# RWKV steps: one bank and one eviction for the 64x64 results of both chunks, and the newer tile first in a round

## The chip, the core and the metric

The kernel runs on one core of a Trainium2 chip. A core has five engines that run their own instruction queues in order: TensorE (matmuls, written PE, its weight loads PEld), VectorE (DVE), ScalarE (ACT), GpSimd (POOL) and SyncE (SP, which issues DMAs). They wait for each other with semaphores. TensorE writes its results to PSUM, eight banks of 128 partitions x 512 fp32; VectorE or ScalarE then move them to SBUF, which is called an eviction here. The metric is the device time of the whole kernel in microseconds; lower is better.

## The reference

Everything is fp32. The model is a mixer block (attention, an RG-LRU, an RWKV-7 recurrence), then two further layers with experts. The change touches the RWKV part alone, for one sequence of 1024 tokens and 4 heads of 64:

```python
def step(state, inp):
    r_t, w_t, k_t, v_t, kk_t, b_t = inp
    sa = jnp.einsum("bhvk,bhk->bhv", state, -kk_t)
    state = (state * w_t[:, :, None, :] + sa[..., None] * b_t[:, :, None, :]
             + v_t[..., None] * k_t[:, :, None, :])
    y_t = jnp.einsum("bhvk,bhk->bhv", state, r_t)
    return state, y_t
...
_, y = lax.scan(step, s0, (tm(rh), tm(wh), tm(kh), tm(vh), tm(kk), tm(bh)))
```

## The kernel before, in words

The recurrence is computed in chunks of 64 tokens (`CH`). Within a chunk it becomes products of 64x64 matrices and the inverse of a triangular one, found by repeated squaring. A tile is 128 tokens, that is two chunks: chunk 0 lies on partitions 0 to 63, chunk 1 on 64 to 127 (`HALVES`). There are eight tiles (`NT`).

A tile goes through 20 steps. Steps 0 to 9 are its front: `ab`, `tok` (0), `p2` (1), `kr` (2), `p4`, `x1` (3), `p8`, `x2` (4), `akv`, `x3` (5), `xt` (6), `q32` (7), `pb` (8), `q64` (9). They do not need the state. Steps 10 to 18 are its back: `x64` (10), `gt`, `u0` (11), `sv0` (12), `dv0`, `ys0` (13), `sv1` (14), `dv1`, `ys1` (15), `yc` (16), `mean` (17), `var` (18), and in step 19 VectorE alone takes the reciprocal of the deviation (L1341) and multiplies by it (L1343). The state passes from chunk to chunk through `sv`, SA (L1304, VectorE), `dv` and the new state (L1315).

`rounds()` (L973) sets the order for TensorE, ScalarE and VectorE alike: in round r = 10 i + s the back step 10 + s of tile i - 1 comes first, then the front step s of tile i. Each of the three engines runs its own function over these rounds: `pe_rwkv` (L1007), `act_rwkv` (L1171), `dve_rwkv` (L1224). While tile 0 is in work, ScalarE and VectorE also run pieces of the RG-LRU (`act_lru`, `dve_lru`), after each step of tile 0.

`by_chunk` (L1016) issues a step's products, for each head q once on the rows of chunk 0 and once on those of chunk 1, each of the two with a PSUM bank of its own. A matmul reads one chunk's rows and writes the same half of the partitions. The bank of chunk 0 and that of chunk 1 are then evicted by two operations on 64 partitions each: `chunk` (L1182, recorded at `copy`, L1180) on ScalarE, `combine` (L1247, recorded at L1252) and `chunk1` (L1254, recorded at L1257) on VectorE. For `p2` and `p4`, which hold two products, ScalarE takes chunk 0 and VectorE chunk 1. `by_parity` (L1039) does `ab` and `kr`; their evictions are L1239 and L1245 (masks).

The banks are two rings, `fr` of four banks for the front and `bk_` of four for the back. A key of a ring gets its bank by its place in FRONT or BACK (L959, L963), and a matmul waits until the key four places earlier is evicted. All matmuls of the stage but `tok` (L1061) are recorded at L202. Each fp32 matmul leaves two records in the trace for the matmul and two for the weight load.

Of the kernel before, what the change touches and what calls it, by code (L numbers as in the profile page):

```python
# [18 lines left out]
NT = T // P  # L19
HD = 64  # L20
AH, AKV = 8, 2
# [4 lines left out]
CH = 64  # L26
# [144 lines left out]
def build(nc, io):  # L171
    ctx = ExitStack()
    with ctx:
# [7 lines left out]
        V, S, G = signal("dve_own"), signal("act_own"), signal("pool_own")  # L181
# [22 lines left out]
        def wait_all(e, points):  # L204
            for point in points:
                e.wait_ge(*point)
# [476 lines left out]
        mN, id64, mT3, mU3 = take(CH), take(CH), take(3, CH), take(3, CH)  # L683
# [264 lines left out]
        def tile_set():  # L948
# [10 lines left out]
        FRONT = [("ab0", "V"), ("ab1", "V"), ("tok0", "S"), ("tok1", "S"), ("p2_0", "S"), ("p2_1", "V"), ("kr0", "V"), ("kr1", "V"),  # L959
# [3 lines left out]
        BACK = [("x64_0", "V"), ("x64_1", "V"), ("gt_0", "S"), ("gt_1", "S"), ("u0_0", "S"), ("u0_1", "S")]  # L963
# [9 lines left out]
        def rounds():  # L973

            for r in range(10 * (NT + 1)):
                i, s = divmod(r, 10)
                if i:
                    yield i - 1, 10 + s
                if i < NT:
                    yield i, s  # L980
# [26 lines left out]
        def pe_rwkv(e):  # L1007
            wait_all(e, after_prep)
            for i, s in rounds():
# [6 lines left out]
                def by_chunk(ring, name, products, *after):  # L1016

                    wait_all(e, after)
                    keys = [(i, f"{name}_{c}") for c in range(2)]
                    for key in keys:  # L1020
                        wait_all(e, ring.free(key))
                    for g, (lhs, rhs) in enumerate(products):
                        for q in range(4):
                            for c, cr in enumerate(HALVES):
                                o = ring.bank[keys[c]][cr, 4 * CH * g + CH * q:4 * CH * g + CH * (q + 1)]
                                m = mm(e, o, lhs(q)[cr], rhs(q)[cr], True, True)
                                if (g, q) == (len(products) - 1, 3):
                                    m.then_inc(*ring.fill(keys[c]))

                def of(t):  # L1030
                    return lambda q: t[:, q, :]
# [3 lines left out]

                def both(name):
                    return [fr.empty((i, f"{name}_{c}")) for c in range(2)]
# [25 lines left out]
                elif s == 1:  # L1063
                    by_chunk(fr, "p2", [(of(NT_), of(N)), (of(N), of(NT_))], fr.empty((i, "ab0")), fr.empty((i, "ab1")))
                elif s == 2:
                    by_parity("kr", [(Kf, Af), (Bf, Rf), (Kf, Rf)])
                elif s == 3:
                    by_chunk(fr, "p4", [(of(PTA), of(PA)), (of(PA), of(PTA))], *both("p2"))
                    by_chunk(fr, "x1", [(of(PA), of(XTa))])
                elif s == 4:  # L1070
                    by_chunk(fr, "p8", [(of(PTB), of(PB))], *both("p4"))
                    by_chunk(fr, "x2", [(of(PB), of(XTb))], *both("x1"))
                elif s == 5:
                    by_chunk(fr, "akv", [(of(AKT), tok(3))], fr.empty((i, "kr1")))
                    by_chunk(fr, "x3", [(of(PA), of(XTa))], *both("p8"), *both("x2"))
                elif s == 6:
                    by_chunk(fr, "xt", [(of(XTb), lambda q: id64)], *both("x3"))
                elif s == 7:
                    by_chunk(fr, "q32", [(of(CT32), of(X_))], *both("xt"))
                elif s == 8:  # L1080
                    by_chunk(fr, "pb", [(of(XTb), of(Q)), (of(Q), of(XTb))], *both("q32"))
                elif s == 9:
                    by_chunk(fr, "q64", [(of(CT64), of(XB))], *both("pb"))
                elif s == 10:
                    by_chunk(bk_, "x64", [(of(Q), of(XTa))], *both("q64"))
                elif s == 11:
                    for c in range(2):
                        e.wait_ge(*bk_.empty((i, f"x64_{c}")))
# [10 lines left out]
                    by_chunk(bk_, "u0", [(of(XTb), of(AKV))], *both("akv"))  # L1099
# [64 lines left out]
        def side(ap, cr, n):  # L1164

            return ap[cr, 0:CH * n].rearrange("p (a b) -> p a b", a=n)

        def flat(ap):
            return ap.rearrange("p a b c -> p (a b) c")

        def act_rwkv(e):  # L1171
            wait_all(e, after_prep)
            for i, s in rounds():
                own = sets[i % 2]
                tk, GT, AKV, U0, Q = (own[n] for n in ("tok", "GT", "akv", "u0", "Q"))
                cols = slice(P * i, P * (i + 1))

                def copy(ring, name, dst, src):
                    e.wait_ge(*ring.full((i, name)))
                    e.activation(dst, src, ACT.Copy, bias=0.0).then_inc(*ring.drain((i, name), "S"))  # L1180

                def chunk(ring, name, c, dst, n):  # L1182
                    copy(ring, f"{name}_{c}", dst[HALVES[c]], side(ring.bank[i, f"{name}_{c}"], HALVES[c], n))

                if s == 0:
                    if i == 1:
                        e.wait_ge(*lru_u.at(2))
                    for half in range(2):
                        copy(fr, f"tok{half}", tk[:, 4 * half:4 * half + 4, :], four(fr.bank[i, f"tok{half}"]))
                elif s == 1:  # L1190
                    chunk(fr, "p2", 0, flat(own["P1"]), 8)
                elif s == 3:
                    chunk(fr, "p4", 0, flat(own["P2"]), 8)
                elif s == 4:
                    for c in range(2):
                        chunk(fr, "p8", c, own["P1"][:, 0], 4)
                elif s == 5:
                    for c in range(2):
                        chunk(fr, "akv", c, AKV, 4)
                elif s == 6:  # L1200
                    for c in range(2):
                        chunk(fr, "xt", c, own["X1"][:, 0], 4)
                elif s in (7, 9):
                    for c in range(2):
                        chunk(fr, "q32" if s == 7 else "q64", c, Q, 4)
                elif s == 11:
                    for c in range(2):
                        copy(bk_, f"gt_{c}", GT[:, :, HALVES[c]], two(bk_.bank[i, f"gt_{c}"], CH))
                    for c in range(2):
                        chunk(bk_, "u0", c, U0, 4)  # L1210
# [12 lines left out]

        def dve_rwkv(e):  # L1224
# [4 lines left out]
            for i, s in rounds():  # L1229
# [17 lines left out]
                def combine(ring, name, dst, src, op, n=4):  # L1247

                    for c, cr in enumerate(HALVES):
                        key = (i, f"{name}_{c}")  # L1250
                        e.wait_ge(*ring.full(key))
                        e.tensor_tensor(dst[cr], src[cr], side(ring.bank[key], cr, n), op).then_inc(*ring.drain(key, "V"))  # L1252

                def chunk1(name, dst):  # L1254
                    key = (i, f"{name}_1")
                    e.wait_ge(*fr.full(key))
                    e.tensor_copy(flat(dst)[HALVES[1]], side(fr.bank[key], HALVES[1], 8)).then_inc(*fr.drain(key, "V"))  # L1257
# [10 lines left out]
                elif s == 1:  # L1268
                    e.wait_ge(*fr.empty((i, "ab1")))
                    e.tensor_tensor(X2[:, 1], own["T3"][:, 0], bc_mid(id64, 4), ALU.add).then_inc(*V.up())  # L1270
                    chunk1("p2", own["P1"])
# [4 lines left out]
                elif s == 3:  # L1276
                    chunk1("p4", own["P2"])
                    e.wait_ge(*V.last())
                    combine(fr, "x1", X1[:, 1], X2[:, 1], ALU.add)
                elif s == 4:  # L1280
                    for c in range(2):
                        e.wait_ge(*fr.empty((i, f"x1_{c}")))
                    combine(fr, "x2", X2[:, 1], X1[:, 1], ALU.add)
                elif s == 5:
                    for c in range(2):
                        e.wait_ge(*fr.empty((i, f"x2_{c}")))
                    combine(fr, "x3", X1[:, 1], X2[:, 1], ALU.add)
                elif s == 8:
                    for c in range(2):
                        e.wait_ge(*fr.empty((i, f"xt_{c}")))  # L1290
                        e.wait_ge(*fr.empty((i, f"x3_{c}")))
                    combine(fr, "pb", flat(X2), flat(X1), ALU.subtract, 8)
                elif s == 10:
                    for c in range(2):
                        e.wait_ge(*fr.empty((i, f"pb_{c}")))
                    combine(bk_, "x64", X1[:, 1], X2[:, 1], ALU.subtract)
                elif s in (12, 14):
                    c = (s - 12) // 2
                    cr = HALVES[c]
                    e.wait_ge(*bk_.empty((i, f"u0_{c}")))  # L1300
# [1725 lines left out]
```

## Time and profile before

| what | us |
|---|---|
| median of 3 runs | 2386.47 (2379.73 to 2386.75) |
| the profiled execution | 2384.51 |
| its span, first to last instruction | 2382.8 |
| TensorE busy | 2136.5 (90%) |
| VectorE busy | 852.3 (36%) |
| ScalarE busy | 580.0 (24%) |
| GpSimd busy | 198.0 (8%) |
| mean granted TensorE clock | 0.940 of full |

The rows further down come from this one profiled execution. Times are microseconds from the span's start unless marked ns. In the view in order of time, like instructions that follow each other are merged: the row has the start, the length from the first start to the last end, the engine, the line, the operation and the count, and in brackets how long the engine stood idle before it and what ended that. Matmuls are pipelined, so a busy TensorE is not TensorE at its peak.

### The profile page before, as it was taken

The page shows a single profiled execution, that of the slowest core. Times are in us where ns is not written, and L with a number is a line of the kernel's source. Part 1 is how long each engine was busy: PE and PEld are TensorE (multiplying, and loading weights), DVE is VectorE, ACT ScalarE, POOL GpSimd, SP SyncE. Part 2 cuts the span into 40 slices and gives each one's busy share as a digit, 9 for nine tenths or more (in the row PEclk, how much of TensorE's full clock was granted, in tenths as well). Part 3 has the DMA queues.
Part 4 walks back from the last instruction along what each step waited for, and adds up shares of the span by engine and source line. Part 5 has one row for each costly group of instructions (what it writes and reads, how often), then busy time and mean ns, then how long its engine had stood idle before and what let it go on. Part 6 is the DMA issues. An engine that isn't in the chain of part 4 may idle for free. (4 is left out here: it accounts for less than half of the span.)

```text
span 2382.8 us, 27540 instructions
## 1 busy us (share of the span) xinstructions
PE 2136.5 (90%) x10876; PEld 1236.1 (52%) x10876; DVE 852.3 (36%) x1873; ACT 580.0 (24%) x1397; POOL 198.0 (8%) x297
## 2 busy tenths in 40 slices
PE   8999999777797949999995999999999949999991
PEld 4545554677444824444443656777764424444440
DVE  1116648766143441111123543443441141112115
ACT  1013334344011301111221433333331111111112
POOL 0000002010242200000001100000000000000002
PEclk9999999799798969999997999999999959999996
DMA  3500000000211147999975100000010057999976
GB/s 124 212 23 36 18 2 3 2 3 3 107 53 40 54 184 293 365 411 377 372 298 191 55 1 1 1 1 1 27 57 27 27 203 295 369 372 370 366 283 239
DMA packets 46200, 349.30 MB, mean 147 GB/s; under 512 B 6256, under 2 KB 6576, under 8 KB 36208
## 3 DMA queue, kind: packets, MB, share of 16 engines
q1 hardware_dynamic: 32176, 296.97, 31.9%
q0 software_dynamic: 13888, 50.47, 6.0%
q8 instruction: 92, 1.51, 0.3%
q14 instruction: 44, 0.36, 0.0%
HBM read 292.82 MB, written 54.59 MB: 146 GB/s over the span
## 5 line engine op out<-in xcount | busy, mean ns | idle before, releaser
L202 PE MATMUL psum<-arena 128*128 128x512 f32 (+7 forms) x9328 | 1976.2, 389 | 147.7 <-DVE arena L1920 25.9
L202 PEld LDWEIGHTS psum<-arena 128*128 128x128 f32 (+3 forms) x9328 | 1062.1, 174 | 992.4 <-issue 842.9
L2051 DVE TENSOR_TENSOR arena<-psum,arena 128x256 f32<-128x256 f32 x64 | 27.2, 425 | 541.0 <-ACT arena L2095 541.0
L2131 POOL DMA_INDIRECT arena<-xn_rows,arena x64 | 60.2, 941 | 819.9 <-PE psum L2018 589.2
L2095 ACT ACTIVATE arena<-psum 128x256 f32<-128x256 f32 x64 | 24.6, 384 | 402.0 <-PE psum L202 402.0
L1472 ACT ACTIVATE arena<-arena 128x1024 f32<-128x1024 f32 x43 | 45.4, 1056 | 259.2 <-DVE arena L2786 101.6
L2699 ACT ACTIVATE arena<-psum,arena 128x1024 f32<-128x1024 f32 (+8 forms) x72 | 50.2, 699 | 188.7 <-DVE arena L2735 188.7
L1180 ACT ACTIVATE arena<-psum 64x256 f32<-64x256 f32 (+4 forms) x176 | 66.0, 389 | 119.1 <-PE psum L202 93.0
L2088 ACT ACTIVATE arena<-psum 128x512 f32<-128x512 f32 x64 | 38.2, 597 | 185.5 <-PE psum L202 185.5
L2018 PE MATMUL psum<-arena 128*128 128x128 f32 x512 | 68.2, 277 | 10.6 <-DMA arena<-xn_rows,arena 10.6
L2118 DVE COPY arena<-psum 128x512 f32<-128x512 f32 x64 | 44.3, 692 | 61.4 <-PE psum L202 61.4
L2018 PEld LDWEIGHTS psum<-arena 128*128 128x128 f32 x512 | 59.3, 144 | 12.0 <-DMA arena<-xn_rows,arena 10.9
L2076 ACT ACTIVATE arena<-psum 128x512 f32<-128x512 f32 x64 | 38.3, 598 | 94.0 <-PE psum L2018 94.0
L2728 DVE TENSOR_TENSOR psum<-psum,arena 128x128 f32<-128x128 f32 (+2 forms) x72 | 20.4, 283 | 103.4 <-PE psum L202 103.1
L2730 DVE TENSOR_REDUCE arena<-psum 128x1 f32<-128x1024 f32 (+8 forms) x72 | 50.8, 706 | 2.5
L1252 DVE TENSOR_TENSOR arena<-arena,psum 64x256 f32<-64x256 f32 (+1 forms) x80 | 37.8, 473 | 36.9 <-PE psum L202 35.3
L2239 DVE SCALAR_TENSOR_TENSOR arena<-arena 128x1024 f32<-128x1024 f32 (+1 forms) x34 | 43.6, 1282 | 20.2 <-DMA arena<-expert_rows,arena 18.7
L2751 DVE COPY arena<-psum 128x512 f32<-128x512 f32 (+3 forms) x48 | 22.8, 490 | 76.0 <-PE psum L2654 75.9
L2245 POOL DMA_INDIRECT arena<-expert_rows,arena x34 | 34.4, 1011 | 178.5 <-issue 125.4
L2654 PE MATMUL psum<-arena 128*128 128x128 f32 x352 | 48.9, 273 | 0.0
L2111 DVE COPY arena<-psum 128x512 f32<-128x512 f32 x64 | 43.6, 681 | 12.4 <-PE psum L2018 12.4
L365 ACT ACTIVATE arena<-psum 128x512 f32<-128x512 f32 (+1 forms) x26 | 15.5, 597 | 128.5 <-PE psum L202 128.5
(286 smaller groups left out, 1290.4 us busy)
## 6 DMA issues: line engine op xcount, KB each, us to landing
arena<-in_w_exp SPq DMA_DIRECT2D x64, 3072.0 KB, 12.3
expert_rows<-arena SPq DMA_DIRECT2D x80, 512.0 KB, 4.0
arena<-in_x SPq DMA_DIRECT2D x16, 512.0 KB, 5.6
xn_rows<-arena SPq DMA_DIRECT2D x16, 512.0 KB, 2.6
arena<-in_w_out SPq DMA_DIRECT2D x8, 512.0 KB, 7.2
arena<-in_w_o SPq DMA_DIRECT2D x1, 4096.0 KB, 13.4
out<-arena SPq DMA_DIRECT2D x8, 512.0 KB, 5.9
arena<-in_rows SPq DMA_DIRECT2D x6, 512.0 KB, 6.5
```

The lines of the kernel that those rows point to most:

```text
L202: return e.matmul(out, lhsT, rhs, start=start, stop=stop, skip_group_check=True)
L1180: e.activation(dst, src, ACT.Copy, bias=0.0).then_inc(*ring.drain((i, name), "S"))
L1472: return e.activation(junk, h[:, s, :], ACT.Square, accum_out=sq_sum[:, s:s + 1])
L2018: m = e.transpose(four(ring.bank[key])[:, k, :], xe[:, P * (4 * hf + k):P * (4 * hf + k + 1)], ident)
L2076: e.activation(y.xt[b % 2][:, 4:8, :], four(y.ex.bank[key]), ACT.Copy, bias=0.0).then_inc(*y.ex.drain(key, "S"))
L2111: e.tensor_copy(y.xt[b % 2][:, 0:4, :], four(y.ex.bank[key])).then_inc(*y.ex.drain(key, "V"))
L2118: e.tensor_copy(y.y[b % 3][:, half_cols(0)], y.ex.bank[key]).then_inc(*y.ex.drain(key, "V"))
L2131: e.indirect_dma_start(out=xe, out_offset=None, in_=xn_dram[:, :], in_offset=bass.IndirectOffsetOnAxis(idx.bitcast(I32)[:, block:block + 1 ...
L2239: e.scalar_tensor_tensor(out=h[0:n, s, :], in0=c[j][0:n, :], scalar=gates[0:n, s, j:j + 1], in1=h[0:n, s, :], op0=ALU.mult, op1=ALU.add).t ...
L2654: m = e.transpose(four(sd.bank[key])[:, j, :], pb[:, kp:kp + P], ident)
L2699: e.activation(pb[0:n, p0:p1], part_bank(key).bank[key][0:n, 0:p1 - p0], ACT.Exp, bias=mx[0:n, 0:1], scale=SCALE, accum_out=rsu[0:n, u:u + ...
L2730: e.tensor_reduce(mx[0:n, u:u + 1], bk[0:n, 0:p1 - p0], AX.X, ALU.max).then_inc(*V.up())
```

## The change

Three things are done. `by_chunk` takes one bank: both chunks' products of a step go to it, chunk 0 to partitions 0 to 63 and chunk 1 to 64 to 127, and one semaphore increment stands on the last matmul. `p2` and `p4` become two keys each, one for each of their two products (`p2a`, `p2b`, `p4a`, `p4b`), as each product now fills a bank's 256 columns on both halves. The evictions take 128 partitions in one operation: `heads` in place of `chunk`, `combine` without its loop, and `second` in place of `chunk1`, which takes the second product. The two rings have 19 keys a tile (28 before) and 18 (20 before). And in a round the front step of the newer tile comes first.

```diff
         def rounds():
             for r in range(10 * (NT + 1)):
                 i, s = divmod(r, 10)
+                if i < NT:
+                    yield i, s
                 if i:
                     yield i - 1, 10 + s
-                if i < NT:
-                    yield i, s
...
                 def by_chunk(ring, name, products, *after):
                     wait_all(e, after)
-                    keys = [(i, f"{name}_{c}") for c in range(2)]
-                    for key in keys:
-                        wait_all(e, ring.free(key))
+                    key = (i, name)
+                    wait_all(e, ring.free(key))
                     for g, (lhs, rhs) in enumerate(products):
                         for q in range(4):
-                            for c, cr in enumerate(HALVES):
-                                o = ring.bank[keys[c]][cr, 4 * CH * g + CH * q:4 * CH * g + CH * (q + 1)]
+                            for cr in HALVES:
+                                o = ring.bank[key][cr, 4 * CH * g + CH * q:4 * CH * g + CH * (q + 1)]
                                 m = mm(e, o, lhs(q)[cr], rhs(q)[cr], True, True)
-                                if (g, q) == (len(products) - 1, 3):
-                                    m.then_inc(*ring.fill(keys[c]))
+                    m.then_inc(*ring.fill(key))
...
-                    by_chunk(fr, "p2", [(of(NT_), of(N)), (of(N), of(NT_))], fr.empty((i, "ab0")), fr.empty((i, "ab1")))
+                    by_chunk(fr, "p2a", [(of(NT_), of(N))], fr.empty((i, "ab0")), fr.empty((i, "ab1")))
+                    by_chunk(fr, "p2b", [(of(N), of(NT_))])
...
-                def chunk(ring, name, c, dst, n):
-                    copy(ring, f"{name}_{c}", dst[HALVES[c]], side(ring.bank[i, f"{name}_{c}"], HALVES[c], n))
+                def heads(ring, name, dst):
+                    copy(ring, name, dst, side(ring.bank[i, name], 4))
...
-                    for c in range(2):
-                        chunk(fr, "p8", c, own["P1"][:, 0], 4)
+                    heads(fr, "p8", own["P1"][:, 0])
...
                 def combine(ring, name, dst, src, op, n=4):
-                    for c, cr in enumerate(HALVES):
-                        key = (i, f"{name}_{c}")
-                        e.wait_ge(*ring.full(key))
-                        e.tensor_tensor(dst[cr], src[cr], side(ring.bank[key], cr, n), op).then_inc(*ring.drain(key, "V"))
-
-                def chunk1(name, dst):
-                    key = (i, f"{name}_1")
+                    key = (i, name)
+                    e.wait_ge(*ring.full(key))
+                    e.tensor_tensor(dst, src, side(ring.bank[key], n), op).then_inc(*ring.drain(key, "V"))
+
+                def second(name, dst):
+                    key = (i, name)
                     e.wait_ge(*fr.full(key))
-                    e.tensor_copy(flat(dst)[HALVES[1]], side(fr.bank[key], HALVES[1], 8)).then_inc(*fr.drain(key, "V"))
+                    e.tensor_copy(dst[:, 1], side(fr.bank[key], 4)).then_inc(*fr.drain(key, "V"))
```

The other steps change in the same way.

## Rows read from the trace of the kernel before

**Rows 1.** Busy time by stretch (columns as its heading says).

```profile
core 0: us, PE busy (x) PEld busy (x) DVE busy (x) ACT busy (x) POOL busy (x), PEclk, DMA share, GB/s
412.20:436.50 24.30, 13.94 (x296) 12.39 (x296) 16.76 (x27) 8.69 (x15) 0.00 (x0) 0.68 0.01 2
436.50:462.00 25.50, 19.10 (x464) 17.58 (x464) 20.36 (x40) 8.98 (x24) 0.00 (x0) 0.83 0.01 3
...
485.10:508.20 23.10, 18.97 (x464) 17.28 (x464) 14.67 (x37) 9.33 (x24) 2.24 (x4) 0.85 0.01 3
...
530.60:551.60 21.00, 16.56 (x464) 14.91 (x465) 14.72 (x37) 8.98 (x24) 2.25 (x4) 1.00 0.01 2
...
595.10:619.30 24.20, 12.65 (x168) 10.95 (x168) 8.45 (x19) 3.93 (x12) 4.48 (x8) 0.50 0.00 1
```

**Rows 2.** In order of time, TensorE, one tile at full clock.

```profile
530.67 0.68 PE L202 MATMUL psum<-arena 64*64 64x64 f32 x16 [1.61 <-DVE arena L1252]
...
532.24 1.15 PE L202 MATMUL psum<-arena 64*64 64x64 f32 x48 [0.88 <-ACT arena L1180]
...
533.32 1.09 PE L1061 MATMUL psum<-arena 128*128 128x128 f32 x8
...
534.34 0.94 PE L202 MATMUL psum<-arena 64*64 64x64 f32 x32
...
535.49 2.05 PE L202 MATMUL psum<-arena 64*64 64x64 f32 x88 [0.21 <-DVE arena L1245]
...
538.03 2.63 PE L202 MATMUL psum<-arena 64*64 64x64 f32 x80 [0.50 <-DVE arena L1304]
...
540.87 0.68 PE L202 MATMUL psum<-arena 64*64 64x64 f32 x16 [0.21 <-DVE arena L1257]
...
541.77 3.61 PE L202 MATMUL psum<-arena 64*64 64x64 f32 x104 [0.22 <-DVE arena L1252]
...
545.72 1.32 PE L202 MATMUL psum<-arena 64*64 64x64 f32 x20 [0.34 <-DVE arena L1252]
...
547.28 2.73 PE L202 MATMUL psum<-arena 64*64 64x64 f32 x52 [0.24 <-ACT arena L1180]
```

**Rows 3.** In order of time, TensorE, the same burst in another tile.

```profile
486.72 1.97 PE L202 MATMUL psum<-arena 64*64 64x64 f32 x48 [0.88 <-ACT arena L1180]
```

**Rows 4.** Groups by line and shape in 530.6 to 551.6 (busy us, mean ns; idle before).

```profile
L1252 DVE TENSOR_TENSOR arena<-arena,psum 64x256 f32<-64x256 f32 x8 | 3.4, 419 | 1.2 <-PE psum L202 1.1
...
L1257 DVE COPY arena<-psum 64x512 f32<-64x512 f32 x2 | 1.4, 694 | 1.0 <-PE psum L202 0.9
L1252 DVE TENSOR_TENSOR arena<-arena,psum 64x512 f32<-64x512 f32 x2 | 1.4, 684 | 2.6 <-PE psum L202 2.6
...
L1180 ACT ACTIVATE arena<-psum 64x256 f32<-64x256 f32 x12 | 4.5, 378 | 5.9 <-PE psum L202 5.7
```

**Rows 5.** Groups by line and shape, operations on 128x256 elsewhere in the kernel.

```profile
L2051 DVE TENSOR_TENSOR arena<-psum,arena 128x256 f32<-128x256 f32 x64 | 27.2, 425 | 541.0 <-ACT arena L2095 541.0
...
L2095 ACT ACTIVATE arena<-psum 128x256 f32<-128x256 f32 x64 | 24.6, 384 | 402.0 <-PE psum L202 402.0
...
L2751 DVE COPY arena<-psum 128x256 f32<-128x256 f32 x8 | 3.4, 425 | 21.3 <-PE psum L2654 21.3
```

**Rows 6.** One line's instructions (ns min/median/max), full clock first, then half.

```profile
L202 PE MATMUL psum<-arena x16: 218/218/267, 540.9 to 541.3; 64*64 64x64 f32 x16
...
L202 PE MATMUL psum<-arena x24: 311/311/365, 602.0 to 603.4; 64*64 64x64 f32 x24
```

**Rows 7.** In order of time, VectorE, reciprocal, then first and last eviction of `ab`.

```profile
530.61 1.75 DVE L1341 RECIPROCAL arena<-arena 128x256 f32<-128x256 f32 x1
...
533.92 0.29 DVE L1239 TENSOR_TENSOR arena<-psum,arena 128x128 f32<-128x128 f32 x1
...
534.79 0.55 DVE L1245 TENSOR_TENSOR arena<-psum,arena 128x384 f32<-128x384 f32 x1
```

**Rows 8.** In order of time, TensorE in the first and the last tile.

```profile
430.99 1.12 PE L202 MATMUL psum<-arena 64*64 64x64 f32 x16 [0.89 <-ACT arena L1180]
...
602.04 1.64 PE L202 MATMUL psum<-arena 64*64 64x64 f32 x24 [0.71 <-DVE arena L1304]
```

More of the change, by code:

```diff
@@ L956, in build @@
         sets.append(tile_set())
-        FRONT = [("ab0", "V"), ("ab1", "V"), ("tok0", "S"), ("tok1", "S"), ("p2_0", "S"), ("p2_1", "V"), ("kr0", "V"), ("kr1", "V"),
[3 rows of a table removed]
-        BACK = [("x64_0", "V"), ("x64_1", "V"), ("gt_0", "S"), ("gt_1", "S"), ("u0_0", "S"), ("u0_1", "S")]
+        FRONT = [("ab0", "V"), ("ab1", "V"), ("tok0", "S"), ("tok1", "S"), ("p2a", "S"), ("p2b", "V"), ("kr0", "V"), ("kr1", "V"),
+                 ("p4a", "S"), ("p4b", "V"), ("x1", "V"), ("p8", "S"), ("x2", "V"), ("akv", "S"), ("x3", "V"), ("xt", "S"), ("q32", "S"),
+                 ("pb", "V"), ("q64", "S")]
+        BACK = [("x64", "V"), ("gt_0", "S"), ("gt_1", "S"), ("u0", "S")]
         for c in range(2):
@@ L1034, in tok @@
                     return lambda q: htok(tk, kind, q)
-                def both(name):
-                    return [fr.empty((i, f"{name}_{c}")) for c in range(2)]
                 def by_parity(name, products):
@@ L1067, in pe_rwkv @@
                 elif s == 3:
-                    by_chunk(fr, "p4", [(of(PTA), of(PA)), (of(PA), of(PTA))], *both("p2"))
+                    by_chunk(fr, "p4a", [(of(PTA), of(PA))], fr.empty((i, "p2a")), fr.empty((i, "p2b")))
+                    by_chunk(fr, "p4b", [(of(PA), of(PTA))])
                     by_chunk(fr, "x1", [(of(PA), of(XTa))])
                 elif s == 4:
-                    by_chunk(fr, "p8", [(of(PTB), of(PB))], *both("p4"))
-                    by_chunk(fr, "x2", [(of(PB), of(XTb))], *both("x1"))
+                    by_chunk(fr, "p8", [(of(PTB), of(PB))], fr.empty((i, "p4a")), fr.empty((i, "p4b")))
+                    by_chunk(fr, "x2", [(of(PB), of(XTb))], fr.empty((i, "x1")))
                 elif s == 5:
                     by_chunk(fr, "akv", [(of(AKT), tok(3))], fr.empty((i, "kr1")))
-                    by_chunk(fr, "x3", [(of(PA), of(XTa))], *both("p8"), *both("x2"))
+                    by_chunk(fr, "x3", [(of(PA), of(XTa))], fr.empty((i, "p8")), fr.empty((i, "x2")))
                 elif s == 6:
-                    by_chunk(fr, "xt", [(of(XTb), lambda q: id64)], *both("x3"))
+                    by_chunk(fr, "xt", [(of(XTb), lambda q: id64)], fr.empty((i, "x3")))
                 elif s == 7:
-                    by_chunk(fr, "q32", [(of(CT32), of(X_))], *both("xt"))
+                    by_chunk(fr, "q32", [(of(CT32), of(X_))], fr.empty((i, "xt")))
                 elif s == 8:
-                    by_chunk(fr, "pb", [(of(XTb), of(Q)), (of(Q), of(XTb))], *both("q32"))
+                    by_chunk(fr, "pb", [(of(XTb), of(Q)), (of(Q), of(XTb))], fr.empty((i, "q32")))
                 elif s == 9:
-                    by_chunk(fr, "q64", [(of(CT64), of(XB))], *both("pb"))
+                    by_chunk(fr, "q64", [(of(CT64), of(XB))], fr.empty((i, "pb")))
                 elif s == 10:
-                    by_chunk(bk_, "x64", [(of(Q), of(XTa))], *both("q64"))
+                    by_chunk(bk_, "x64", [(of(Q), of(XTa))], fr.empty((i, "q64")))
                 elif s == 11:
-                    for c in range(2):
-                        e.wait_ge(*bk_.empty((i, f"x64_{c}")))
+                    e.wait_ge(*bk_.empty((i, "x64")))
                     keys = [(i, f"gt_{c}") for c in range(2)]
@@ L1098, in pe_rwkv @@
                                 m.then_inc(*bk_.fill(keys[c]))
-                    by_chunk(bk_, "u0", [(of(XTb), of(AKV))], *both("akv"))
+                    by_chunk(bk_, "u0", [(of(XTb), of(AKV))], fr.empty((i, "akv")))
                 elif s in (12, 14):
@@ L1162, in pe_rwkv, with side @@
                     m.then_inc(*bk_.fill(key))
-        def side(ap, cr, n):
-            return ap[cr, 0:CH * n].rearrange("p (a b) -> p a b", a=n)
+        def side(ap, n):
+            return ap[:, 0:CH * n].rearrange("p (a b) -> p a b", a=n)
         def flat(ap):
@@ L1190, in act_rwkv @@
                 elif s == 1:
-                    chunk(fr, "p2", 0, flat(own["P1"]), 8)
+                    heads(fr, "p2a", own["P1"][:, 0])
                 elif s == 3:
-                    chunk(fr, "p4", 0, flat(own["P2"]), 8)
+                    heads(fr, "p4a", own["P2"][:, 0])
                 elif s == 4:
-                    for c in range(2):
-                        chunk(fr, "p8", c, own["P1"][:, 0], 4)
+                    heads(fr, "p8", own["P1"][:, 0])
                 elif s == 5:
-                    for c in range(2):
-                        chunk(fr, "akv", c, AKV, 4)
+                    heads(fr, "akv", AKV)
                 elif s == 6:
-                    for c in range(2):
-                        chunk(fr, "xt", c, own["X1"][:, 0], 4)
+                    heads(fr, "xt", own["X1"][:, 0])
                 elif s in (7, 9):
-                    for c in range(2):
-                        chunk(fr, "q32" if s == 7 else "q64", c, Q, 4)
+                    heads(fr, "q32" if s == 7 else "q64", Q)
                 elif s == 11:
@@ L1208, in act_rwkv @@
                         copy(bk_, f"gt_{c}", GT[:, :, HALVES[c]], two(bk_.bank[i, f"gt_{c}"], CH))
-                    for c in range(2):
-                        chunk(bk_, "u0", c, U0, 4)
+                    heads(bk_, "u0", U0)
                 elif s in (13, 15):
@@ L1270, in dve_rwkv @@
                     e.tensor_tensor(X2[:, 1], own["T3"][:, 0], bc_mid(id64, 4), ALU.add).then_inc(*V.up())
-                    chunk1("p2", own["P1"])
+                    second("p2b", own["P1"])
                 elif s == 2:
@@ L1276, in dve_rwkv @@
                 elif s == 3:
-                    chunk1("p4", own["P2"])
+                    second("p4b", own["P2"])
                     e.wait_ge(*V.last())
@@ L1280, in dve_rwkv @@
                 elif s == 4:
-                    for c in range(2):
-                        e.wait_ge(*fr.empty((i, f"x1_{c}")))
+                    e.wait_ge(*fr.empty((i, "x1")))
                     combine(fr, "x2", X2[:, 1], X1[:, 1], ALU.add)
                 elif s == 5:
-                    for c in range(2):
-                        e.wait_ge(*fr.empty((i, f"x2_{c}")))
+                    e.wait_ge(*fr.empty((i, "x2")))
                     combine(fr, "x3", X1[:, 1], X2[:, 1], ALU.add)
                 elif s == 8:
-                    for c in range(2):
-                        e.wait_ge(*fr.empty((i, f"xt_{c}")))
-                        e.wait_ge(*fr.empty((i, f"x3_{c}")))
+                    e.wait_ge(*fr.empty((i, "xt")))
+                    e.wait_ge(*fr.empty((i, "x3")))
                     combine(fr, "pb", flat(X2), flat(X1), ALU.subtract, 8)
                 elif s == 10:
-                    for c in range(2):
-                        e.wait_ge(*fr.empty((i, f"pb_{c}")))
+                    e.wait_ge(*fr.empty((i, "pb")))
                     combine(bk_, "x64", X1[:, 1], X2[:, 1], ALU.subtract)
@@ L1299, in dve_rwkv @@
                     cr = HALVES[c]
-                    e.wait_ge(*bk_.empty((i, f"u0_{c}")))
+                    e.wait_ge(*bk_.empty((i, "u0")))
                     for par in range(2):
```

3 rows, old and new, of the table FRONT are left out of this document.

## Prediction

> **What bounds the kernel now.** Read the page's head first: the span is 2382.8 us, and the change touches one stage of it. The views by line and in order of time place that stage, RWKV, from 412.2 to 619.3 us: 207 us, 8.7% of the span, so nothing outside can move except by being shifted. Next read the busy times by stretch, one stretch per tile, cut where the tile's `q64` matmuls start [rows 1]. A tile that runs beside its neighbour takes 21.0 to 25.5 us; the first (front only) and the last (back only) take 24.3 and 24.2 us. No engine is full: in the stretch from 530.6, at clock 1.00, TensorE shows 16.56 of 21.00 us and VectorE 14.72, while a tile's ScalarE work is 8.98.
>
> Then read one such tile in order of time [rows 2]. TensorE runs in bursts, and each bracket names an eviction of this stage as what ended the gap: 1.61, 0.88, 0.21, 0.50, 0.21, 0.22, 0.34 and 0.24 us, together 4.21 us in the 21.0 us from one `q64` to the next. The largest two are a tile's `pb` (VectorE, two 64x512 operations) ahead of `q64`, and `q64` (ScalarE, two 64x256) ahead of `x64`. So the stage is bound by a chain matmuls, eviction, matmuls, in which in-order TensorE stands still because the other tile's work is queued behind the waiting instruction, not ahead of it.
>
> Two tile lengths exist because of the clock. A burst of 48 records takes 1.15 us at full clock [rows 2] and 1.97 us after the same gap in another tile [rows 3]; that tile's stretch has mean clock 0.85 and 23.1 us [rows 1]. The clock level falls to the lower of its two (1.2 instead of 2.4 GHz) around the two long gaps.
>
> **Part 1: one eviction instead of two.** A matmul here leaves two records. Thirteen results per tile change. Two evictions of 64x256 on ScalarE cost 378 ns each, on VectorE 419; one `pb` half 64x512 costs 684; the 64x512 copy of `p2`, `p4` 694 on VectorE [rows 4]. The price of 128 partitions stands elsewhere in the trace: ScalarE copy 128x256 384 ns, VectorE add 128x256 425, VectorE copy 128x256 425 [rows 5]; so partitions cost nothing, columns do. For 128x512 on VectorE I take the 684 of 64x512. A pair on ScalarE then shrinks from about 0.78 to 0.38 us, on VectorE from 0.87 to 0.43, `pb` from 1.40 to 0.69, and `p2`/`p4` (side by side on two engines) from 0.70 to 0.43. Each lies on the chain where a gap follows it, and nowhere else. VectorE's work per tile falls from 14.7 to about 14.7 - 4 x 0.42 - 0.71 - 2 x 0.27 = 11.8 us, below TensorE's.
>
> **Part 2: order.** In a round the younger tile's step now goes first on all three queues, and in the first round of ten `ab` and `tok` stand between `q64` and `x64`; `p2` stands between `x64` and `gt`; `dv`/`ys` between `x1` and `p8`; `yc` between `xt` and `q32`; and so on. Nothing is added; 464 matmul records a tile stay. No DMA is moved. What is queued behind each wait changes, so I walk a tile.
>
> Lengths of the bursts at full clock [rows 2]: 16 records take 0.68 us of which one record's own 218 ns [rows 6] is the tail, so a step with one product issues for (0.68 - 0.22)/15 = 31 ns a record, 0.50 us; `pb`, `p2`, `p4` 1.0 us. `ab` and `kr` come to 14 to 15 ns a record from the 48 and 88 record bursts (0.45 and 0.72 us), `gt` 0.22, `dv` with `ys` 0.80 (the 80 burst less 56 other records), `tok` 1.03 (533.32 to 534.34), `yc` 0.75, `mean` and `var` 0.5 each. Sum 14.0 us. From a step's first matmul to its eviction is 0.68 us for 16 records and 1.2 for 32; from an eviction's end to the next matmul 0.10 to 0.15.
>
> The walk from `q64` at 0. `ab` issues at 0.50, `tok` 0.95 to 1.98, `x64` to 2.48: `q64`'s eviction (0.68 to 1.06) is covered, the 0.88 gap is gone. VectorE meanwhile is the new late one. The previous tile's reciprocal (1.75 us, L1341 [rows 7]) waits for `var`, which now comes after `pb`, so it starts at about 0.6; with L1343 it ends at 2.7; only then come the four operations that evict `ab` (1.42 us [rows 7]), to 4.1. `p2` waits for them until 4.2: **a new gap of 1.7 us**, with `gt`, `u0`, `kr` and `sv0` queued behind it. `p2` to 5.2, `gt`, `u0` to 5.95, `kr` to 6.67, `sv0` to 6.8, `p4` and `x1` to 8.3. `dv0` needs SA, which VectorE now does behind `kr` (6.85 to 7.85), until 8.33: gap 0.15 where it was 0.50. `dv0`, `ys0` to 9.25 cover the evictions of `p4` and `x1` (to 9.2): both 0.2 gaps gone. `p8`, `x2`, `sv1`, `akv` to 10.87; `x3` waits 0.1 for `x2`; `dv1`, `ys1` to 12.28 cover `x3`; `xt`, `yc` to 13.53 cover `xt`; `q32` to 14.03; `mean` waits 0.3 for L1330; `pb` to 15.82, full at 16.0, evicted by 16.7; `var` waits 0.3 for L1217 and ends at 16.6; next `q64` at 16.8. Gaps: 2.8 us instead of 4.2 plus the tails that now overlap. Checked the same way, the old order gives 14.0 + 4.2 + 0.95 of short waits hidden inside bursts + about 1.7 of tails = 20.85 against 21.0 measured. I add 0.4 for what a walk misses: **17.2 us a tile**.
>
> **The sum.** The seven stretches between 436.5 and 595.1 are 158.6 us, mean 22.65. At full clock seven would be 146.6; of the 12 us excess some 3 are the LRU scans on VectorE in the stretch from 436.5 (25.5 us [rows 1]), 9 the clock. After: 7 x 17.2 = 120.4; LRU 4, as it sits on the engine that is now late; clock 6, since a 1.7 us gap remains but the 0.88 behind the `pb` gap is gone. That is 130.4, a saving of 28.2. First tile: alone and a plain chain (a gap of 0.89 before each step [rows 8]); shorter by 0.44 each for `x1`, `x2`, `x3`, 0.40 each for `xt`, `q32`, and `q64` into `x64`, 0.71 for `pb`, 0.27 each for `p2`, `p4` is 3.8; VectorE's LRU work covers a little: 3.5. Last tile: `x64` and little else, 0.8. Together 32.5 us. The profiled execution took 2384.5 us (1.7 outside its span), the median of the runs is 2386.5, 2.0 more: 2384.5 - 32.5 + 2.0 = **2354 us**, 1.4% less.
>
> **The rule that speaks against it.** No row shows two row groups of TensorE writing one bank in turn: all steps of before give each row group its own bank. The nearest row is `dv`, one row group, one bank, both halves of partitions: in a burst of 24 records at the low clock with `ys` it comes to (1.64 - 0.31)/23 = 58 ns a record, against (1.12 - 0.31)/15 = 54 for a two-bank step at the same clock [rows 6, 8]. So writing one bank in turn need not cost, and I take 31 ns at full clock. From below: `ab` shows 14 ns, so 17 ns x 2048 records = 35 us more could be gained. From above: strictly one after another is 218 ns [rows 6], 2048 x 0.187 = 383 us lost. The Trainium skill, TensorEngine Tiling (Array Packing), Restrictions and Gotchas, says that different row tiles cannot use one PSUM bank at the same time; by it the halves would no longer overlap. The Trainium skill, PSUM — Partial Sum Buffer, on bank collisions, allows different column tiles on disjoint partitions in one bank, which these also are, and so gives the forecast. No run here shows either yet.
>
> **Rivals.** (a) **The bank serialises**, the slower case: the two halves of a pair take turns and the pitch doubles, +31 ns. A tile then is 17.2 + 256 x 0.031 less about 1 of covered gaps = 24.2 us, 7 x 24.2 + 4 = 173 against 158.6, the first tile +3: 2386.5 + 14 + 3 = 2404 us. It decides from about +16 ns a record (32.5 / 2048). For it: no row excludes it; against it: `dv`. 7%. (b) **VectorE's queue is the bound**: `kr` ahead of SA and the reciprocal ahead of `ab` cost more than walked, 19 us a tile, all of today's clock loss: 133 + 4 + 9 = 146, saving 12.6 + 4: 2370 us. For it: the reciprocal is the longest operation and always queued there; against: VectorE has 5 us to spare a tile. 20%. (c) **The clock stays up** throughout and the walk is exact: 7 x 16.8 + 4 = 121.6, saving 37 + 4.3: 2345 us. 18%. (d) The gaps only change place (each covered wait returns behind another step) and only the evictions' own saving in the first and last tile is left: 2382 us, no change; against it is that the walk finds cover of 0.5 us or more for six of eight gaps. 4%. (e) The pitch falls towards `ab`'s; VectorE's 11.8 us and the same 1.7 us gap keep a tile above 15.5: 2340 us or a little less. 5%. The forecast has the other 46%.
>
> **How the numbers follow.** The range takes in (b), (c), the forecast and most of (e): 2338 to 2374; outside stay (a), (d) and the lowest part of (e). About 0.3%, 7 us, is what a measurement can tell: faster is the forecast, (b), (c), (e) at 0.89; same (d) and the mildest part of (a) at 0.04; slower 0.07.
>
> **What would show it.** In the profile after: 64x256 and 64x512 evictions gone, 128x256 ones of 0.38 and 0.43 us and 128x512 of 0.69 in place; TensorE's gap ended by L1252-like lines before `q64` down to about 0.2 and none before `x64`; a gap over 1 us before `p2` ended by the masks' line; bursts of 16 at 0.68 us at full clock (1.2 or more would be rival (a)); tiles of 17 to 18 us; clock near 1. I am wrong if the pitch changes, if VectorE has idle time while TensorE waits for it, or if a tile stays above 19 us.

## The result

The changed kernel takes 2345.2 us (2343.62 to 2347.21, 4 runs) against 2383.1 us (2372.3 to 2386.75, 4 runs) for the kernel before on the same chip: a ratio of 0.9848, with a 95% interval of 0.9826 to 0.9870, so 31 to 41 us less. The forecast was 2354 us, 32.5 us less, with a range of 2338 to 2374. The profiled execution has a span of 2343.3 us, 39.5 less than before.

The stage, from its first 64x64 matmul to the load that waits for its end, is where it went. Two rows of after, in order of time:

```profile
414.40 0.69 PE L202 MATMUL psum<-arena 64*64 64x64 f32 x32 [0.94 <-DVE arena L832]
...
581.54 3.94 SPq L1402 DMA_DIRECT2D arena<-in_w_out  x8
```

That is 167.1 us. The same two rows of before give 207.0:

```profile
412.26 0.69 PE L202 MATMUL psum<-arena 64*64 64x64 f32 x32 [0.93 <-DVE arena L832]
...
619.29 4.07 SPq L1416 DMA_DIRECT2D arena<-in_w_out  x8
```

The 39.9 us between them are the whole difference of the spans: the part ahead of the stage is 2.1 us longer in after, the part behind it 1.7 shorter. Busy time by stretch of after, cut as in [rows 1]:

```profile
core 0: us, PE busy (x) PEld busy (x) DVE busy (x) ACT busy (x) POOL busy (x), PEclk, DMA share, GB/s
414.30:434.10 19.80, 12.44 (x296) 10.98 (x296) 13.57 (x23) 6.68 (x11) 0.00 (x0) 0.77 0.01 2
434.10:454.50 20.40, 18.17 (x474) 16.60 (x476) 16.96 (x34) 6.54 (x18) 0.00 (x0) 0.89 0.01 3
454.50:471.80 17.30, 15.42 (x462) 14.25 (x457) 11.62 (x31) 6.45 (x19) 2.32 (x4) 1.00 0.01 4
...
506.20:523.60 17.40, 15.84 (x464) 14.69 (x464) 11.52 (x32) 6.64 (x19) 2.31 (x4) 1.00 0.02 4
...
541.40:559.40 18.00, 15.64 (x464) 14.53 (x464) 11.67 (x32) 6.59 (x19) 2.31 (x4) 1.00 0.01 3
559.40:581.70 22.30, 10.94 (x168) 9.20 (x168) 7.98 (x19) 3.53 (x11) 4.49 (x8) 0.62 0.01 1
```

A tile takes 17.1 to 18.0 us where it took 20.9 to 23.1, and the one with the LRU work 20.1 where it took 25.5 (each from one `q64` to the next). From 454.5 to 559.4 us the clock is at its full level. VectorE's work in a tile fell from 14.7 to 11.5 us, ScalarE's from 9.0 to 6.6, and TensorE still has 464 records. One tile of after in order of time:

```profile
505.52 0.69 DVE L1242 TENSOR_TENSOR arena<-arena,psum 128x512 f32<-128x512 f32 x1 [0.76 <-PE psum L202]
506.05 0.47 ACT L1211 ACTIVATE arena<-psum,arena 128x256 f32<-128x256 f32 x1 [0.84 <-PE psum L202]
...
506.26 1.15 PE L202 MATMUL psum<-arena 64*64 64x64 f32 x48 [0.25 <-DVE arena L1242]
506.56 1.75 DVE L1327 RECIPROCAL arena<-arena 128x256 f32<-128x256 f32 x1 [0.35 <-ACT arena L1211]
506.99 0.39 ACT L1176 ACTIVATE arena<-psum 128x256 f32<-128x256 f32 x1 [0.46 <-PE psum L202]
...
507.34 1.09 PE L1056 MATMUL psum<-arena 128*128 128x128 f32 x8
...
508.35 0.43 DVE L1329 TENSOR_TENSOR arena<-arena 128x256 f32<-128x256 f32 x1
...
508.37 0.68 PE L202 MATMUL psum<-arena 64*64 64x64 f32 x16
508.69 0.28 DVE L1230 TENSOR_TENSOR arena<-psum,arena 128x128 f32<-128x128 f32 x1
...
509.55 0.55 DVE L1236 TENSOR_TENSOR arena<-psum,arena 128x384 f32<-128x384 f32 x1
...
510.20 13.16 PE L202 MATMUL psum<-arena 64*64 64x64 f32 x392 [1.15 <-DVE arena L1236]
...
511.39 0.42 DVE L1247 COPY arena<-psum 128x256 f32<-128x256 f32 x1 [0.54 <-PE psum L202]
```

Of the eight gaps of [rows 2] one is left, and a new one has come. The gap ahead of `q64` is 0.25 us (1.61 before), there is none ahead of `x64`. 1.15 us now lie ahead of `p2`: VectorE does the reciprocal and its product until 508.8, and then `ab`'s four evictions until 510.1. The other 392 records go through in one burst in this tile. The tile is 506.26 to 523.62, 17.36 us.

### The profile page after: what moved, and what is told of

Same layout as the page of the kernel before. It is cut to its first block and busy times, and to the rows that moved or that the text cites. A ratio compares the mean times of both kernels' runs of the same rounds, so it can differ in the third digit from the quotient of the medians.

```text
span 2343.3 us, 27331 instructions
## 1 busy us (share of the span) xinstructions
PE 2118.2 (90%) x10876; PEld 1221.1 (52%) x10876; DVE 826.4 (35%) x1833; ACT 560.0 (24%) x1349; POOL 198.8 (8%) x297
## 5 line engine op out<-in xcount | busy, mean ns | idle before, releaser
L202 PEld LDWEIGHTS psum<-arena 128*128 128x128 f32 (+3 forms) x9328 | 1050.3, 170 | 967.7 <-issue 840.2
L2074 ACT ACTIVATE arena<-psum 128x512 f32<-128x512 f32 x64 | 38.3, 598 | 185.5 <-PE psum L202 185.5
L1176 ACT ACTIVATE arena<-psum 128x256 f32<-128x256 f32 (+3 forms) x128 | 45.7, 369 | 90.7 <-PE psum L202 80.6
L2062 ACT ACTIVATE arena<-psum 128x512 f32<-128x512 f32 x64 | 38.3, 598 | 93.9 <-PE psum L2004 93.9
L379 DVE TENSOR_TENSOR arena<-psum,arena 128x512 f32<-128x512 f32 x16 | 10.9, 689 | 87.5 <-ACT arena L360 87.4
```

The lines of the kernel that those rows point to most:

```text
L202: return e.matmul(out, lhsT, rhs, start=start, stop=stop, skip_group_check=True)
L2062: e.activation(y.xt[b % 2][:, 4:8, :], four(y.ex.bank[key]), ACT.Copy, bias=0.0).then_inc(*y.ex.drain(key, "S"))
```

## The experiments

The length of the stage is read as above, from the one profiled execution of each kernel. Two executions of the changed kernel differ by 1.4 us in it; the kernel before was profiled once. "Seven tiles" is from the first `q64` to the eighth; the first of the seven holds the LRU work. The three medians of before are those beside which the changed kernel, e1 to e4, and e5 to e8 were timed, so times of different groups are compared by their ratios or by the stage.

| kernel | time us | ratio to before, 95% interval | stage us | seven tiles us |
|---|---|---|---|---|
| before | 2383.1, 2385.1, 2381.9 | 1 | 207.0 | 158.6 |
| changed | 2345.2 | 0.9848 (0.9826 to 0.9870) | 167.1 | 125.4 |
| e5, changed again | 2343.8 | 0.9841 (0.9822 to 0.9860) | 165.7 | 124.7 |
| e1, order alone | 2365.3 | 0.9916 (0.9897 to 0.9934) | 188.1 | 140.0 |
| e2, evictions alone | 2345.7 | 0.9832 (0.9812 to 0.9853) | 168.7 | 127.5 |
| e3, chunk by chunk | 2354.2 | 0.9876 (0.9856 to 0.9895) | 177.4 | 132.8 |
| e4, reciprocal moved | 2338.1 | 0.9804 (0.9784 to 0.9823) | 158.1 | 118.2 |
| e6, evictions and reciprocal | 2346.2 | 0.9850 (0.9833 to 0.9866) | 167.6 | 128.5 |
| e7, e4 and SA first | 2334.0 | 0.9801 (0.9779 to 0.9823) | 158.1 | 117.9 |
| e8, order and reciprocal | 2366.4 | 0.9932 (0.9916 to 0.9949) | 186.3 | 138.8 |

### e1: the new order alone

On the kernel before:

```diff
+                if i < NT:
+                    yield i, s
                 if i:
                     yield i - 1, 10 + s
-                if i < NT:
-                    yield i, s
```

> The kernel before with the swap of the two steps in a round alone: two banks and two 64-partition evictions a step stay. My theory (order and evictions each take a share, and the shares overlap, since a gap covered by other work can't also be shortened): a tile of about 19 us at full clock, no gap between q64 and x64, still one of about 0.9 us between pb and q64 and one before p2; the first and the last tile as before. About 2366 us, 16 to 20 us under the kernel before. Rival 1 (the order does everything and the evictions are hidden anyway): the same time as the changed kernel, 2345 to 2348. Rival 2 (the evictions do everything): the time of the kernel before, 2380 to 2386.

Measured: 2365.3 us, and tiles of 19.2 to 19.9 us at full clock, about 19 as expected. TensorE in one of them, 19.5 us long:

```profile
500.34 1.15 PE L202 MATMUL psum<-arena 64*64 64x64 f32 x48 [0.96 <-DVE arena L1252]
501.45 1.09 PE L1061 MATMUL psum<-arena 128*128 128x128 f32 x8
502.48 0.68 PE L202 MATMUL psum<-arena 64*64 64x64 f32 x16
504.08 7.66 PE L202 MATMUL psum<-arena 64*64 64x64 f32 x248 [0.92 <-DVE arena L1245]
512.05 1.68 PE L202 MATMUL psum<-arena 64*64 64x64 f32 x40 [0.31 <-DVE arena L1252]
```

The wait for `x64` is gone, the one for `pb` is down from 1.61 to 0.96, and the new one of 0.92 ahead of `p2` has come. With the long evictions the order is worth 207.0 - 188.1 = 18.9 us. Both rivals are excluded.

### e2: the evictions alone

On the changed kernel:

```diff
+                if i:
+                    yield i - 1, 10 + s
                 if i < NT:
                     yield i, s
-                if i:
-                    yield i - 1, 10 + s
```

> The changed kernel with the old order of the two steps in a round. My theory: the gaps before q64 shrinks from 1.60 to about 0.9 us, before x64 from 0.88 to about 0.5, and those of 0.2 to 0.3 us vanish: a tile of 18.3 us at full clock, first tile 4 to 5 us shorter, as in the changed kernel; about 2356 us. Rival 1 (order does everything): 2378 to 2386, the first tile's gain alone. Rival 2 (evictions do everything): the time of the changed kernel.

Measured: 2345.7 us, the time of the changed kernel, so rival 2 is what happened and my 2356 was wrong. The two gaps that I had priced came out as expected (0.89 and 0.48 us), the tile did not. TensorE in one tile:

```profile
489.13 0.68 PE L202 MATMUL psum<-arena 64*64 64x64 f32 x16 [0.89 <-DVE arena L1242]
490.29 1.15 PE L202 MATMUL psum<-arena 64*64 64x64 f32 x48 [0.48 <-ACT arena L1176]
491.37 1.09 PE L1056 MATMUL psum<-arena 128*128 128x128 f32 x8
492.39 11.11 PE L202 MATMUL psum<-arena 64*64 64x64 f32 x356
503.86 1.79 PE L202 MATMUL psum<-arena 128*128 128x128 f32 x36 [0.35 <-ACT arena L1208]
506.54 0.68 PE L202 MATMUL psum<-arena 64*64 64x64 f32 x16 [0.89 <-DVE arena L1242]
```

Two of the eight gaps of [rows 2] are left, both shorter. The six of 0.2 to 0.5 us are gone, and one is new: 0.35 us ahead of `var`, where the same operation of ScalarE had held TensorE up by less than 0.1 us before. The gaps now sum to 1.72 us instead of 4.21, and the tile is 17.41 us, not the 18.3 I had worked out. So the gaps give 2.5 of the 3.5 us by which the tile is shorter. The other microsecond is in TensorE's busy time, 15.59 us in this tile against 16.56 in that of [rows 2]. A burst's last record shows 218 ns where the records inside it follow each other at 31, so each gap that goes takes some 0.19 us of busy time with it; for five gaps fewer that makes 0.9 us (an estimate). My 18.3 had left these tails out. The prediction's walk had them in.

The short evictions are worth 207.0 - 168.7 = 38.3 us, and the order on top of them 1.6 to 3.0. Those few are in the tile with the LRU work (22.1 us here, at clock 0.83, against 20.1 in both executions of the changed kernel, at 0.89 and 0.90). The other six tiles take 105.3 us here and 105.3 and 104.7 in the changed kernel, so in them the new order is worth 0.7 us at most.

### e3: chunk by chunk in the one bank

```diff
-                        for q in range(4):
-                            for cr in HALVES:
+                        for cr in HALVES:
+                            for q in range(4):
                                 o = ring.bank[key][cr, 4 * CH * g + CH * q:4 * CH * g + CH * (q + 1)]
```

> The changed kernel, but a step issues the four products of chunk 0 and then the four of chunk 1, where it took them in turn; same bank, same count. It asks why the shared bank costs nothing. Theory A (the two row groups do overlap, though they share a bank): without the turns the pitch goes from 31 to some 60 ns a record, a burst of 16 from 0.68 to about 1.15 us at full clock, 256 x 0.03 = 8 us a tile less what fills gaps, so 2390 to 2400 us. Theory B (in these steps the two halves never overlapped, before either, so there was nothing to lose): burst 0.68 us and 2343 to 2349 us, as the changed kernel.

Measured: 2354.2 us, between the two. `q32` in the first tile at half clock, and `x64` in a tile at full clock:

```profile
428.37 1.60 PE L202 MATMUL psum<-arena 64*64 64x64 f32 x16 [0.47 <-ACT arena L1176]
...
475.78 0.96 PE L202 MATMUL psum<-arena 64*64 64x64 f32 x16
```

The burst of 16 is 0.96 us against 0.68, a pitch of (0.96 - 0.22)/15 = 49 ns against 31; at half clock (1.60 - 0.31)/15 = 86 against 54. Theory A had 1.15 us for the burst and 2390 us or more, theory B no change; both missed. So the two row groups gain from taking turns, by a factor of 1.6 in a step of 16 records rather than 2, and they do so while they write one bank. Whether that gain is the matmuls' overlap or that of the weight loads, no run took apart. The forecast's rival (a) is settled all the same: the burst of 16 is 0.68 us with two banks [rows 2] and 0.68 us with one.

By the Trainium skill, TensorEngine Tiling (Array Packing), Restrictions and Gotchas, the halves should have lost that overlap; the measurement decides against it for halves that write different partitions. The Trainium skill, PSUM — Partial Sum Buffer, says, on bank collisions, that different column tiles may use one bank at the same time on disjoint partitions, which the burst of 0.68 us agrees with; the same passage says, as the other page does, that different row tiles may not. The halves here are both, and the prediction named only the first of the two.

### e4: the reciprocal moved away from `ab`

```diff
-                elif s == 19:
-                    ...
-                    e.reciprocal(dev, dev).then_inc(*V.up())
-                    e.wait_ge(*V.last())
-                    e.tensor_tensor(y2, y2, dev, ALU.mult).then_inc(*y_norm.up())
+                if s == 19 and i == NT - 1:
+                    for part in range(3):
+                        normalise(i, part)
+                elif s in (11, 15, 17) and i:
+                    normalise(i - 1, (11, 15, 17).index(s))
```

`normalise` does the reciprocal of one half (128x128) as parts 0 and 1 and the product as part 2.

> The changed kernel, with VectorE's step 19 (the reciprocal of 1.75 us and the product of 0.43) taken off its place ahead of the eviction of ab: one half of the reciprocal of the tile before after p2b's eviction, the other after dv1's, the product after L1321's. Same work. My theory (the 1.15 us gap before p2 is the reciprocal's): that gap falls to about 0.2 us or none, a tile goes from 17.35 to about 16.3 us, about 2338 us. Rival (VectorE is late in any case, and the half reciprocal ahead of kr's eviction turns into a longer wait for SA): gap moves to before dv0, 2343 to 2348 us.

Measured: 2338.1 us, as my theory had it. Its six tiles behind the LRU one take 16.0 to 16.8 us. One of the shortest:

```profile
503.76 1.15 PE L202 MATMUL psum<-arena 64*64 64x64 f32 x48 [0.25 <-DVE arena L1254]
504.84 1.09 PE L1056 MATMUL psum<-arena 128*128 128x128 f32 x8
505.04 0.29 DVE L1242 TENSOR_TENSOR arena<-psum,arena 128x128 f32<-128x128 f32 x1 [1.34 <-PE psum L202]
...
505.87 13.40 PE L202 MATMUL psum<-arena 64*64 64x64 f32 x406
...
508.09 0.94 DVE L1227 RECIPROCAL arena<-arena 128x128 f32<-128x128 f32 x1
509.20 1.02 DVE L1248 TENSOR_TENSOR arena<-psum,arena 128x384 f32<-128x384 f32 x2 [0.17 <-PE psum L202]
```

`ab` is evicted as soon as it is there, `p2` no longer waits, and 1.15 us of gap and 0.2 more are gone: the tile is 503.76 to 519.74, 15.98 us. It is the first kernel here that beats the changed one: the stage is 7.6 to 9.0 us shorter, 6.5 to 7.2 of them in the seven tiles and 1.8 to 1.9 in the last one, which has clock 0.70 instead of 0.62.

### e5: the changed kernel again

No edit.

> The changed kernel once more, as it is, to stand beside the next three on one chip. All theories: 2343 to 2348 us.

Measured: 2343.8 us, stage 165.7.

### e6: short evictions, old order, reciprocal moved

The edit of e4 on the kernel of e2.

> The short evictions with the old order (as in e2) and the reciprocal taken apart and moved as in e4. Theory (with the old order the reciprocal has free time on VectorE and is on no path; only the new order puts it ahead of the eviction of ab): no gain, 2343 to 2348 us, a tile of 17.4 us. Rival (VectorE's reciprocal costs the same in either order, and the order itself is worth nothing): as e4, 2336 to 2340.

Measured: 2346.2 us, stage 167.6 against 168.7 in e2. No gain that can be told, as the theory had it, but the tile is not the expected 17.4 us: the six behind the LRU one take 17.8 to 18.2. The gaps of 0.89, 0.48 and 0.35 us stand as in e2, and one has come that e2 does not have:

```profile
480.13 1.94 PE L202 MATMUL psum<-arena 64*64 64x64 f32 x36 [0.40 <-DVE arena L1254]
```

The second half of the reciprocal (VectorE, from 478.85 for 0.95 us) stands there ahead of the eviction of `x3`, for which `xt` waits. So the six tiles are 2.3 us longer than in e2, while the tile with the LRU work is 1.3 us shorter and the last one 2.0, that one at clock 0.70 instead of 0.56. What the run shows is that no gap of e2 was the reciprocal's. It does not show what a better place for it would bring in the old order.

### e7: e4, with SA ahead of the masks of `kr` on VectorE

```diff
+            def state_first():
+                turns_ = list(rounds())
+                for k in range(len(turns_) - 1):
+                    if turns_[k][1] == 2 and turns_[k + 1][1] == 12:
+                        turns_[k:k + 2] = turns_[k + 1], turns_[k]
+                return turns_
-            for i, s in rounds():
+            for i, s in state_first():
```

> e4, and in round 2 of ten VectorE alone does SA of the older tile ahead of the masks of kr (the other engines keep the new order). Theory (in e4 dv0 waits for SA, which stands behind 1.0 us of masks, the dip in TensorE's records near 510.9 us of e4): a tile falls from 16.0 to about 15.7 us, 2335 to 2337 us. Rival (the masks then are late for x1's bank, or the next wait takes its place): no change against e4, 2337 to 2339, or up to 2 us slower.

Measured: 2334.0 us, but the stage is 158.1 us, to the tenth that of e4. The 4 us between the times, and 5.6 between the spans, lie outside the stage (it begins at 411.1 us here and at 414.8 in e4), and the ratios to before are 0.9804 and 0.9801. So the edit did nothing: the rival holds, though 2334.0 us is below both expected ranges. SA comes 0.7 us sooner (5.70 us after `q64`, 6.37 in e4) and TensorE then waits for the masks instead:

```profile
504.88 0.48 DVE L1309 SCALAR_TENSOR_TENSOR arena<-psum,arena 64x128 f32<-64x128 f32 x2 [0.43 <-PE psum L202]
...
505.29 1.00 DVE L1255 TENSOR_TENSOR arena<-psum,arena 128x384 f32<-128x384 f32 x2
...
505.89 9.23 PE L202 MATMUL psum<-arena 64*64 64x64 f32 x240 [0.18 <-DVE arena L1255]
```

### e8: long evictions, new order, reciprocal moved

The edit of e4 on the kernel of e1.

> The kernel before (two banks, two evictions a step) with the new order and with the reciprocal apart and moved as in e4. It asks what the new order is worth when nothing stands in its way, without the short evictions. Theory (the order's worth was held back by the reciprocal): a tile goes from 19.2 us in e1 to about 18.2, 2357 to 2360 us. Rival (VectorE has too little free time with the long evictions, 14.7 us of 19): 2362 to 2367, as e1.

Measured: 2366.4 us, stage 186.3 against 188.1 in e1: the rival. One tile:

```profile
483.22 4.63 PE L202 MATMUL psum<-arena 64*64 64x64 f32 x168
...
487.10 1.02 DVE L1257 TENSOR_TENSOR arena<-psum,arena 128x384 f32<-128x384 f32 x2
488.04 0.47 DVE L1316 SCALAR_TENSOR_TENSOR arena<-psum,arena 64x128 f32<-64x128 f32 x2
...
488.27 3.71 PE L202 MATMUL psum<-arena 64*64 64x64 f32 x96 [0.42 <-DVE arena L1257]
...
492.65 1.50 PE L202 MATMUL psum<-arena 64*64 64x64 f32 x40 [0.67 <-ACT arena L1180]
```

The gap ahead of `p2` is gone here too, but VectorE, with 14.5 us of work in a tile of 19.2, is in one unbroken row from 484.0 to 488.5, and the wait comes back ahead of `x1` and `x3`.

## Why the prediction was right, point by point

**What bounds the stage.** Right: the whole gain is in the stage, and TensorE's gaps in the tile shown went from 4.2 to 1.4 us.

**The evictions' prices.** Right. At 128 partitions the rows of after show 0.39 and 0.42 us for 256 columns and 0.69 for 512, as [rows 5] and [rows 4] had it. VectorE's tile was put at 11.8 us and is 11.5.

**The walk.** The tile was put at 17.2 us and is 17.36. The new gap ahead of `p2` was foreseen, with its cause. Put at 1.7 us, it is 1.15: the reciprocal starts 0.30 us after `q64`, not 0.6, and `x64`'s last 0.2 us count as busy; `p2` starts 3.94 us after `q64` where the walk had 4.2. From there to the next `q64` it is 13.42 us where the walk had 12.6, although its small waits of 0.1 to 0.3 us show as no gap in this tile. So the walk's bursts were too short in sum, and the 0.4 us added for what a walk misses made up half of that.

**The clock.** Mis-sized. Six microseconds were left for it and four for the LRU. Of the 125.4 us of the seven tiles, 7 x 17.36 = 121.5 are the plain tiles, so 3.9 are left for all else: 2.7 in the tile with the LRU work, at clock 0.89, and 1.1 in the other six, at 1.00. Of the 33.2 us that the seven tiles lost, 7 x (20.94 - 17.36) = 25.1 are the shorter tile at full clock, and the other 8.1 are clock and LRU.

In e2 too, with gaps of 0.89 and 0.48 us, and in e1, with 0.96 and 0.92, the clock is 1.00 from the second of the seven tiles to the last `q64`. In the kernel before, with gaps of 1.61 and 0.88, four of the same six tiles have 0.85 to 0.92, but the two from 530.6 to 573.5 us stay at 1.00 with the same gaps. So the prediction's sentence that the level falls around the two long gaps holds for some tiles and not for others. That shorter gaps keep the clock up is what these rows suggest; no run took the clock by itself.

**First and last tile.** Mis-sized too: both gained more than forecast. The first went from 24.3 to 19.7 us (4.6, put at 3.5), with clock 0.77 instead of 0.68, and the last from 24.1 to 22.1 (2.1, put at 0.8), with 0.62 instead of 0.50. With the seven tiles (33.2, put at 28.2) this makes the 39.9 us against 32.5.

**Where the reasons were wrong.** The time was right, but Part 2 gave the order a share that it does not have. The four cases stand side by side as stage times: long evictions, old order 207.0 and new 188.1; short evictions, old order 168.7 and new 165.7 to 167.1. The order's 18.9 us are real only where the evictions are long. Where they are short, it removes 0.64 + 0.48 + 0.35 us of gaps a tile and puts 1.15 us ahead of `p2`. With the reciprocal moved as well, it is worth 167.6 - 158.1 = 9.5 us (e6 to e4), some 2.3 of which e6 lost by its own new gap. So the order is not worthless: in the changed kernel the wait for the reciprocal cancels what it gains. The walk had both halves of this, but it was made for the new order alone. I never walked the old order with short evictions, and so took the new order to be needed for the gain. The sentence that fell short is that TensorE stands still "because the other tile's work is queued behind the waiting instruction". The order alone does take gaps away (e1), but at six of the eight gaps the old queue runs through as soon as the evictions are short (e2).

**The rivals.** (a) is excluded by the equal bursts and by e3. (b), VectorE's queue as the bound, was right in kind: moving the reciprocal gives 8 us (e4), and only with both parts of the change in place (e6, e8). Its price, 19 us a tile, was not. (c) was nearest to the time, 2345 us, in part by luck: the clock stayed up in six of the seven tiles, but the tile is 17.36 us and not 16.8, and the first and last tile made up for it. (d) and (e) did not occur; a burst of 16 is 0.68 us before and after.

**What stays open.** Why the pitch of the 64x64 steps is 31 ns while `ab` and `kr` go at 14 to 15 was not settled. The depth of the two bank rings changes together with the evictions in every run (19 keys a tile in the front's ring where there were 28), so its share is not taken apart. Each of the eight gaps of [rows 2] ends with an operation whose result the waiting matmuls read, which speaks for the evictions' length; that is argued and not shown. And some tiles of after are 0.5 to 0.7 us longer than others around gaps that no row explains:

```profile
549.49 9.74 PE L202 MATMUL psum<-arena 64*64 64x64 f32 x259 [0.85 <-issue]
```

## What to carry to other kernels

In these rows an eviction of 128 partitions costs what one of 64 does (0.42 us for 256 columns on VectorE). Where a chain runs from matmul to eviction and back, joining the two halves of a step therefore halves the eviction's part of the chain; with what it gave back in clock, that was worth 38 of 40 us here. Before crediting two edits of one change, walk each alone as well as both: two ways to cover the same gap do not add up. After a reordering look for the longest operation that now stands ahead of an urgent one in an in-order queue; cutting it in two and moving the halves was worth another 8 us here. The same places in the old order brought nothing, since there one half landed ahead of another urgent eviction (e6). When you count what a closed gap is worth, count the tail of the burst ahead of it too: about 0.19 us each here.

## What the runs showed of the hardware

Two row groups of TensorE that write different halves of the partitions of one bank in turn go as fast as with a bank each: 0.68 us for 16 records in both. Taking them one chunk after the other costs 49 ns a record instead of 31 at full clock, and 86 instead of 54 at half: alternation is worth a factor of 1.6 in a step of 16 records. On VectorE a reciprocal takes 1.75 us for 128x256 and 0.94 us for 128x128, where an addition of 128x256 takes 0.42.
